# FFN1's pair stage: each product's token highs and lows in one 512-column matmul, and its modulation chunks on GpSimd

## The chip, the cores and the metric

The kernel runs on one NeuronCore of a Trainium2 chip. The metric is the device time of one execution in microseconds (us); lower is better. The inputs lie in HBM in float32.

## What is computed

The kernel is one layer of a diffusion backbone over 256 latent and 256 context tokens with 2048 channels. Two parts matter here. The first feed-forward network, for latent and context tokens with the same weights (inner size 5632, so 44 blocks of 128 rows):

```python
def swiglu(h, w_in, w_out):
    g, u = jnp.split(h @ w_in, 2, axis=-1)
    return (jax.nn.silu(g) * u) @ w_out

m_lat = (jax.nn.silu(c) @ ada_w[l] + ada_b[l]).reshape(b, N_MOD, 1, d)
x = x + 0.5 * m_lat[:, 2] * swiglu(modulate(rms_norm(x, norm1_g[l]), m_lat[:, 0], m_lat[:, 1]), ffn1_w_in[l], ffn1_w_out[l])
```

And the modulation vectors: a product of one vector silu(c) with ada_w (2048 x 18432), of which the later parts are formed little by little beside other work.

## The kernel before, in words

**Precision.** A float32 operand is split into a high part (float32r) and a low part, the rest. A product is three matmuls: weight high by token high, weight high by token low, weight low by token high (`three`, lines 1536 to 1540). ScalarE (ACT) makes the highs by a copy, VectorE (DVE) the lows by a subtraction.

**The stage.** FFN1's first layer has 44 blocks. Blocks 0 to 7 are done in the plain way. Blocks 8 to 43 (`for k in range(FIRST_S, PAIRS)`) are the pair stage, 36 rounds, each called a pair k here: gate and up of both token groups by a scheme of Strassen's kind with seven products (P1, P5, P6, P3, P7, P2, P4) in place of eight. Each product has 8 contraction tiles of 128 and 256 token columns: `pair_product` (line 1635) issues 8 x 3 matmuls of 128x256. Its weights are half slabs of 128x1024: ACT makes the high (`form_high_half`, line 1045), DVE the low (`half_low`, line 2455). Four half slabs of room exist, so the high of product n waits until product n-4 is done. P5 and P6 need weight sums that DVE forms in place (`w_sum`, line 2459, twice a pair), P7 and P4 weight sums that two accumulating DMAs issued by GpSimd form (`sums_added`, lines 862 and 865).

**Banks.** A pair has three PSUM banks x, y, z, and pairs alternate between two sets. x takes P1, then P6, P7 and P4 on top; z takes P5, then P3; y takes P2. Between them results are saved: `pair_keep` on ACT (line 1052) copies x after P1, z after P5 and x after P6, and PE waits for the first copy before P6, for the second before P3, for the third before P7. DVE's `up_ctx` (line 2467) reads x after P7, and PE waits for it before P4. `up_lat` (2472) and `gate_lat` (2476) read z and y. `pair_silu` (1060, 1062) applies SiLU to the two gates, and `pair_gate` (2482) multiplies gate and up into the activation, which GpSimd stores to DRAM (`act_store`, 856).

**Chunks.** Beside it DVE works through `chunk_step` (line 2315): a chunk is 128x1024 of ada_w, multiplied by one column of silu(c) and added to `accl`, one scalar_tensor_tensor. The stage has 96 chunks, 3, 3, 2 and 3 in four pairs, and so on (`S_CHUNKS`), over 35 pairs: 26 pairs with three, 9 with two. Sixteen chunks make a round, whose sums `take_turn`, `take_reduce` and `take_total` fold. Chunks are loaded by SP into three places; the load of a chunk waits for `chunk_free` of the one three before.

**Order.** All orders are written out by hand. In a pair DVE does: half_low 0, up_ctx of the pair before, w_sum, half_low 1, w_sum, gate_lat of the pair before, half_low 2, half_low 3, pair_gate of the pair before, then chunk and half_low in turn for 4, 5, 6, then up_lat. GpSimd's queue holds, per pair: the DMA for P7 (waits for the first w_sum of this pair), the DMA for P4 (waits for half_low 2), the store of the pair before (waits for pair_gate). SP's queue holds four half-slab loads for pair k+2 and the chunk loads between them.

Of the kernel before, what the change touches and what calls it, by code (L numbers as in the profile page):

```python
# [14 lines left out]
F32R = mybir.dt.float32r  # L15
# [5 lines left out]
P = 128  # L21
D = 2048
KT = D // P
# [105 lines left out]
def build(nc, x, c, ctx, c_ctx, ada_w, ada_b, norm1_g, ffn1_w_in, ffn1_w_out, norm2_g,  # L129
# [22 lines left out]
    def sm(name, shape, dt=F32):  # L152
# [7 lines left out]
    hh = at("hh", [P, 2, KT, LAT], F32R, o_hh)  # L160
    hl = at("hl", [P, 2, KT, LAT], F32R, o_hl)
# [5 lines left out]
              for part, n in enumerate(("ah", "al")))  # L167
    fhs, fls = ([at(f"{n}{k}", [P, HALF, LAT], F32R, o + part * 8 * KB) for k, o in enumerate((o_xl, o_xl + 16 * KB, o_a))]
                for part, n in enumerate(("fhs", "fls")))
# [197 lines left out]
    p7_summed, p4_summed = far_loaded, nfb_loaded  # L367
    lat_done, lat_out, LAT_DONE = xra_ready, xrv_ready, 8
# [150 lines left out]
    with block:  # L519
# [323 lines left out]
        def _(pool):  # L843
# [43 lines left out]
        def _(se):  # L887
# [166 lines left out]
            def pair_silu(k):  # L1054
                se.wait_ge(slab_used, prod(k, 6) + 1)
# [4 lines left out]
                nc.scalar.activation(sg[:, LAT:TOK], pair_banks(k)[0][:, 0:LAT], ACT.Silu).then_inc(a_x, 1)  # L1060
                se.wait_ge(a_c11, k - FIRST_S + 1)
                nc.scalar.activation(sg[:, 0:LAT], sg[:, 0:LAT], ACT.Silu).then_inc(a_sg, 1)

            for k in range(FIRST_S, PAIRS):
# [11 lines left out]
                pair_keep(k, 1, tv[:, 1, :], at_z, a_p5)  # L1076
                form_high_half(k, 5)
                pair_keep(k, 2, tv[:, 0, :], at_x, a_u2)
# [21 lines left out]
            act_high(1)  # L1100
            pair_silu(PAIRS - 1)
# [430 lines left out]
        def _(pe):  # L1532
# [102 lines left out]
            def pair_product(k, pos, bank_, first, last):  # L1635
# [4 lines left out]
                for t in range(HALF):  # L1640
                    if name in ("P1", "P2", "P4"):
                        part, t0 = {"P1": (0, 0), "P2": (0, HALF), "P4": (1, HALF)}[name]
                        xh_ap, xl_ap = hh[:, part, t0 + t, :], hl[:, part, t0 + t, :]
                    elif name == "P7":
                        xh_ap, xl_ap = hh[:, 1, t, :], hl[:, 1, t, :]
                    else:
                        f = ("P5", "P6", "P3").index(name)
                        xh_ap, xl_ap = fhs[f][:, t, :], fls[f][:, t, :]
# [1478 lines left out]
```

## Time and profile before

| | us |
|---|---|
| median of 3 runs (2681.79 to 2682.47) | 2681.8 |
| the profiled execution's own time | 2683.84 |
| its span, first to last instruction | 2682.0 |
| PE busy in the span | 2632.7 |
| DVE busy | 2134.1 |
| ACT busy | 1216.8 |
| GpSimd (POOL) busy | 93.7 |

PE is TensorE's matmuls, PEld its weight loads, DVE is VectorE, ACT ScalarE, POOL GpSimd, SP the queue that loads. A row of the timeline has the start from the span's begin, the duration, engine, line of the kernel, operation, output and input tile, shapes, and in brackets how long the engine had been idle and who released it. Durations of operations that follow each other overlap a little at the ends, so what one costs in a stream is read from start to start. The pair stage lies at about 287 to 1016 us.

### The profile page before, as it was taken

How to read it: one execution, taken by the hardware profiler on the slowest of the kernel's cores; microseconds unless marked ns; L12 is line 12 of the kernel's file. 1: busy time of each engine (PE TensorE's matmuls, PEld its weight loads, DVE VectorE, ACT ScalarE, POOL GpSimd, SP SyncE). 2: the span in 40 equal slices, each digit the busy share in tenths (PEclk: the TensorE clock that was granted, in tenths of full speed). 3: DMA queues.
4: the chain of work that ended last, by engine and by line, in shares of the span. 5: the costliest groups of instructions: out<-in, count | busy, mean ns of one | idle time of the engine just before them, and what ended most of it. 6: DMA issues, size and time to landing. Idle time of an engine off the chain costs nothing.

```text
span 2682.0 us, 37985 instructions
## 1 busy us (share of the span) xinstructions
PE 2632.7 (98%) x15293; PEld 2327.4 (87%) x15293; DVE 2134.1 (80%) x2328; ACT 1216.8 (45%) x1399; POOL 93.7 (3%) x131
## 2 busy tenths in 40 slices
PE   5999999999999999999999999999999999999998
PEld 4778999999999998888888988888988888888887
DVE  6869878788787877899797877586688888888866
ACT  6642344444444443231175543465465455555543
POOL 0000111111111110000000000000000000000000
PEclk9999999999999999999999999999999999999999
DMA  9967699999999888667584585442455555556463
GB/s 309 295 199 211 182 245 249 230 249 250 231 232 258 231 232 289 210 226 243 187 279 135 137 263 189 136 132 79 141 177 194 194 194 197 203 204 206 168 220 125
DMA packets 428939, 558.71 MB, mean 208 GB/s; under 512 B 22274, under 2 KB 280696, under 8 KB 428024
## 3 DMA queue, kind: packets, MB, share of 16 engines
q1 hardware_dynamic: 414156, 504.64, 58.4%
q0 software_dynamic: 14384, 51.92, 10.0%
q8 instruction: 104, 1.70, 0.3%
q14 instruction: 43, 0.35, 0.0%
q10 hardware_dynamic: 252, 0.10, 0.0%
HBM read 505.22 MB, written 13.63 MB: 193 GB/s over the span
## 4 chain that ended last, share of the span: by engine, by line
PE 87%; DVE 4%; ACT 1%; issue 1%; DMA 0%; ACTq 0%; DVEq 0%
PE py L1538 14%; PE py L1540 14%; PE py L1539 14%; PE pg L1538 3%; PE pg L1539 3%; PE pg L1540 3%; PE py L2071 3%; PE py L2073 3%; PE py L2072 3%; PE two L2013 2%; PE two L2015 2%; PE two L2014 2%; PE pu L2052 1%; PE pu L2054 1%; PE pu L2053 1%; PE pu L1538 1%
## 5 line engine op out<-in xcount | busy, mean ns | idle before, releaser
L2455 DVE TENSOR_TENSOR wl<-raw,wh 128x1024 fp32r<-128x1024 f32 x252 | 307.8, 1222 | 111.7 <-ACT wh L1045 111.5
L1045 ACT ACTIVATE wh<-raw 128x1024 fp32r<-128x1024 f32 x252 | 265.7, 1055 | 288.7 <-DVE raw L2459 228.0
L2176 DVE TENSOR_TENSOR wl<-raw,wh 128x2048 fp32r<-128x2048 f32 x101 | 231.1, 2288 | 124.4 <-ACT wh L902 124.2
L1538 PE MATMUL py<-ah,wh 128*128 128x512 f32 (+1 forms) x720 | 277.2, 385 | 0.3 <-issue 0.3
L1539 PE MATMUL py<-al,wh 128*128 128x512 f32 (+1 forms) x720 | 276.8, 384 | 0.0
L1540 PE MATMUL py<-ah,wl 128*128 128x512 f32 (+1 forms) x720 | 276.8, 384 | 0.0
L902 ACT ACTIVATE wh<-raw 128x2048 fp32r<-128x2048 f32 x100 | 190.7, 1912 | 189.0 <-PE py L1540 84.6
L1538 PE MATMUL py<-hh,wh 128*128 128x256 f32 (+1 forms) x752 | 226.1, 301 | 1.8 <-DVE hl L2253 1.0
L1539 PE MATMUL py<-hl,wh 128*128 128x256 f32 (+1 forms) x752 | 224.8, 299 | 0.0
L1540 PE MATMUL py<-hh,wl 128*128 128x256 f32 (+1 forms) x752 | 224.8, 299 | 0.0
L1538 PE MATMUL py<-fhs,wh 128*128 128x256 f32 x720 | 204.0, 283 | 0.4 <-DVE wl L2455 0.4
L1539 PE MATMUL py<-fls,wh 128*128 128x256 f32 x720 | 203.8, 283 | 0.0
L1540 PE MATMUL py<-fhs,wl 128*128 128x256 f32 x720 | 203.8, 283 | 0.0
L1096 ACT ACTIVATE wh<-raw 128x2048 fp32r<-128x2048 f32 x44 | 84.3, 1916 | 256.5 <-PE py L1540 256.4
L2315 DVE SCALAR_TENSOR_TENSOR accl<-chunk,cs,accl 128x1024 f32<-128x1024 f32 x150 | 191.9, 1280 | 7.4 <-DMA chunk<-in_ada_w 2.6
L1445 ACT ACTIVATE wh<-sraw 128x2048 fp32r<-128x2048 f32 x63 | 121.0, 1920 | 163.5 <-PE py L2073 59.4
L2945 DVE TENSOR_TENSOR wl<-raw,wh 128x2048 fp32r<-128x2048 f32 x70 | 160.0, 2286 | 35.3 <-ACT wh L1445 35.3
L2945 DVE TENSOR_TENSOR wl<-sraw,wh 128x2048 fp32r<-128x2048 f32 x63 | 144.1, 2287 | 50.3 <-ACT wh L1445 50.3
L1538 PEld LDWEIGHTS py<-ah,wh 128*128 128x128 f32 x720 | 135.3, 188 | 28.0 <-issue 0.9
L1538 PE MATMUL pg<-hh,wh 128*128 128x256 f32 (+1 forms) x528 | 158.1, 299 | 0.8 <-DVE tv L2467 0.6
L1540 PEld LDWEIGHTS py<-ah,wl 128*128 128x128 f32 x720 | 135.3, 188 | 26.8
L1539 PEld LDWEIGHTS py<-al,wh 128*128 128x128 f32 x720 | 135.3, 188 | 26.7
(516 smaller groups left out, 7124.9 us busy)
## 6 DMA issues: line engine op xcount, KB each, us to landing
raw<-in_ffn_w_out SPq DMA_DIRECT2D x84, 1024.0 KB, 5.2
chunk<-in_ada_w SPq DMA_DIRECT2D x160, 512.0 KB, 5.5
raw<-in_ffn_w_in SPq DMA_DIRECT2D x144, 512.0 KB, 7.5
raw<-in_ffn_w_in SPq DMA_DIRECT2D x58, 1024.0 KB, 5.1
sraw<-in_ffn_w_in SPq DMA_DIRECT2D x40, 1024.0 KB, 5.1
raw<-raw POOLq DMA_DIRECT2D x72, 512.0 KB, 5.8
raw<-in_ada_w SPq DMA_DIRECT2D x64, 512.0 KB
raw<-in_mix_w_in SPq DMA_DIRECT2D x30, 1024.0 KB
```

Source lines behind the costliest of these rows:

```text
L902: nc.scalar.activation(wh[:, slot % 2, :], raw[:, slot, :], ACT.Copy).then_inc(wh_ready, 1)
L1045: nc.scalar.activation(wh[:, slot, o:o + 1024], s_half(k, S_SRC[name]), ACT.Copy).then_inc(wh_ready, 1)
L1096: nc.scalar.activation(wh[:, j % 2, :], raw[:, slot, :], ACT.Copy).then_inc(wh_ready, 1)
L1445: nc.scalar.activation(whs[ring(i, name)], src, ACT.Copy).then_inc(wh_ready, 1)
L1538: mm(out_ap, w[0], xh_ap, start=first, stop=False, skip_group_check=True)
L1539: mm(out_ap, w[0], xl_ap, start=False, stop=False, skip_group_check=True)
L1540: return mm(out_ap, w[1], xh_ap, start=False, stop=last, skip_group_check=True)
L2071: mm(banks[k][:], xh_ap, w_h, start=(first and t == 0), stop=False)
L2176: tt(wl[:, slot % 2, :], raw[:, slot, :], wh[:, slot % 2, :].bitcast(F32), ALU.subtract).then_inc(wl_ready, 1)
L2315: ins = stt(a[:], chunks[PLACES[c]], cs[:, t, k:k + 1], a[:], ALU.mult, ALU.add)
L2455: tt(wl[:, slot, o:o + 1024], s_half(k, S_SRC[forms(k)[pos]]), wh[:, slot, o:o + 1024].bitcast(F32), ALU.subtract).then_inc(wl_ready, 1)
L2945: tt(wls[slot], src, whs[slot].bitcast(F32), ALU.subtract).then_inc(wl_ready, 1)
```

## The change

**Matmuls.** The high and low tokens of each operand become one tensor (`hhl`, `fhl`) at the same addresses, so that one access pattern reaches both. For each contraction tile `pair_product` issues two matmuls in place of three: weight high by [token high, token low] into all 512 columns of the bank, and weight low by token high into columns 0 to 255. The result is then the sum of the bank's two halves.

**Reads of the banks.** ACT's copies now take the right half; DVE then adds the left half to the copy (`both_halves`: keep_p1, keep_p5, keep_u2, gate_ctx) and releases PE. up_ctx, up_lat and gate_lat become two operations each with a wait between them. SiLU is one 512-column activation of both gates, after both are complete.

**Chunks.** The 96 chunks of the stage go to GpSimd: a tensor_scalar in place, a wait on its own semaphore, a tensor_tensor into `accl`. They stand in GpSimd's queue after the pair's store. The folding of a round stays on DVE, one pair later.

```diff
-    hh = at("hh", [P, 2, KT, LAT], F32R, o_hh)
-    hl = at("hl", [P, 2, KT, LAT], F32R, o_hl)
+    hhl = at("hhl", [P, 2, 2, KT, LAT], F32R, o_hh)
+    hh, hl = hhl[:, 0], hhl[:, 1]
...
+    fhl = [at(f"fhl{k}", [P, 2, HALF, LAT], F32R, o) for k, o in enumerate((o_xl, o_xl + 16 * KB, o_a))]
+    fhs, fls = ([f[:, part] for f in fhl] for part in range(2))
...
+            def chunk_step(c):
+                t = c % KT
+                pool.wait_ge(chunk_loaded[SIGNAL[c]], CHUNK_BASE[SIGNAL[c]] + 16 * LOADS[c])
+                pool.wait_ge(chunk_free, c + 1)
+                if t == 0:
+                    pool.wait_ge(sums_ready, (TAKEN[c // KT] - 1) * 5 + 1)
+                    ins = nc.gpsimd.tensor_scalar(accl[:], chunks[PLACES[c]], cs[:, 0, 0:1], None, ALU.mult)
+                else:
+                    nc.gpsimd.tensor_scalar(chunks[PLACES[c]], chunks[PLACES[c]], cs[:, t, 0:1], None, ALU.mult).then_inc(pool_chain, 1)
+                    pool.wait_ge(pool_chain, POOL0 + c - KT + 1 - c // KT)
+                    ins = nc.gpsimd.tensor_tensor(accl[:], accl[:], chunks[PLACES[c]], ALU.add)
+                ins.then_inc(chunk_free, 1)
             for k in range(FIRST_S, PAIRS):
                 sums_added(k)
                 act_store(k - 1)
+                for c in S_CHUNKS[k - FIRST_S]:
+                    chunk_step(c)
...
-            def pair_keep(k, pos, dst, src, ready):
+            def pair_keep(k, pos, dst, src):
                 se.wait_ge(slab_used, prod(k, pos) + 1)
-                nc.scalar.activation(dst, src[:, 0:LAT], ACT.Copy).then_inc(ready, 1)
+                nc.scalar.activation(dst, src[:, LAT:TOK], ACT.Copy).then_inc(kept, 1)
...
+                pair_keep(k, 6, sg[:, LAT:TOK], pair_banks(k)[0])
+
+            def pair_silu(k):
                 se.wait_ge(a_c11, k - FIRST_S + 1)
-                nc.scalar.activation(sg[:, 0:LAT], sg[:, 0:LAT], ACT.Silu).then_inc(a_sg, 1)
+                se.wait_ge(a_x, k - FIRST_S + 1)
+                nc.scalar.activation(sg[:], sg[:], ACT.Silu).then_inc(a_sg, 1)
...
                 if k > FIRST_S:
+                    keep_gate(k - 1)
+                form_high_half(k, 3)
+                if k > FIRST_S:
                     pair_silu(k - 1)
-                form_high_half(k, 3)
-                pair_keep(k, 0, p1a[:], at_x, a_p1)
+                pair_keep(k, 0, p1a[:], at_x)
...
-                    ins = three(bank_[:, 0:LAT], w, xh_ap, xl_ap, first and t == 0, t == HALF - 1)
+                    mm(pair(bank_[:]), w_h, both, start=(first and t == 0), stop=False, skip_group_check=True)
+                    ins = mm(bank_[:, 0:LAT], w_l, both[:, 0, :], start=False, stop=(t == HALF - 1), skip_group_check=True)
...
-                tt(tv[:, 1, :], tv[:, 1, :], pair_banks(k)[0][:, 0:LAT], ALU.subtract).then_inc(a_v, 1)
+                x_ = pair_banks(k)[0]
+                link(tt(tv[:, 1, :], tv[:, 1, :], x_[:, 0:LAT], ALU.subtract))
+                tt(tv[:, 1, :], tv[:, 1, :], x_[:, LAT:TOK], ALU.subtract).then_inc(a_v, 1)
...
+            def both_halves(k, n, dst, src, ready):
+                ve.wait_ge(kept, KEPT + 4 * (k - FIRST_S) + n)
+                tt(dst, src[:, 0:LAT], dst, ALU.add).then_inc(ready, 1)
...
                     gate_lat(k - 1)
-                    for c_ in span[:-3]:
-                        chunk_step(c_)
+                    for c_ in S_CHUNKS[k - FIRST_S - 1]:
                         if ends_round(c_):
                             take_turn(c_, 0)
                     half_low(k, 2)
...
+                    gate_ctx(k - 1)
                     half_low(k, 3)
                     pair_gate(k - 1)
...
+                    for n in range(3):
+                        (keep_p1, keep_p5, keep_u2)[n](k)
                         half_low(k, 4 + n)
```

## Rows read from the trace of the kernel before

**Rows 1.** The page: the span, and busy time by engine.
```profile
span 2682.0 us, 37985 instructions
PE 2632.7 (98%) x15293; PEld 2327.4 (87%) x15293; DVE 2134.1 (80%) x2328; ACT 1216.8 (45%) x1399; POOL 93.7 (3%) x131
```

**Rows 2.** Windows: stretch, length, busy by engine (instructions), granted clock, DMA share, GB/s.
```profile
320.00:860.00 540.00, 540.00 (x4503) 540.00 (x4502) 434.94 (x477) 233.62 (x321) 61.73 (x81) 1.00 0.94 243
...
40.00:80.00 40.00, 32.29 (x144) 24.57 (x143) 30.88 (x38) 26.13 (x21) 0.00 (x0) 0.96 0.88 289
```

**Rows 3.** Timeline of DVE, from one pair_gate to the next, the middle left out.
```profile
837.51 0.68 DVE L2482 TENSOR_TENSOR act<-sg,tv 128x512 f32<-128x512 f32 x1
838.12 1.28 DVE L2315 SCALAR_TENSOR_TENSOR accl<-chunk,cs,accl 128x1024 f32<-128x1024 f32 x1
...
848.84 0.42 DVE L2467 TENSOR_TENSOR tv<-tv,py 128x256 f32<-128x256 f32 x1 [0.57 <-PE py L1540]
849.18 1.22 DVE L2459 TENSOR_TENSOR raw<-raw 128x1024 f32<-128x1024 f32 x1
851.52 1.23 DVE L2455 TENSOR_TENSOR wl<-raw,wh 128x1024 fp32r<-128x1024 f32 x1 [1.13 <-ACT wh L1045]
852.66 1.22 DVE L2459 TENSOR_TENSOR raw<-raw 128x1024 f32<-128x1024 f32 x1
853.80 0.42 DVE L2476 TENSOR_TENSOR sg<-py,p1a 128x256 f32<-128x256 f32 x1
855.01 1.23 DVE L2455 TENSOR_TENSOR wl<-raw,wh 128x1024 fp32r<-128x1024 f32 x1 [0.79 <-ACT wh L1045]
856.53 1.23 DVE L2455 TENSOR_TENSOR wl<-raw,wh 128x1024 fp32r<-128x1024 f32 x1 [0.30 <-ACT wh L1045]
857.67 0.68 DVE L2482 TENSOR_TENSOR act<-sg,tv 128x512 f32<-128x512 f32 x1
```

**Rows 4.** Timeline of GpSimd (POOL), the same pair.
```profile
838.50 0.58 POOL L856 DMA_DIRECT2D act_scratch<-act  x1 [1.28 <-DVE act L2482]
850.69 0.86 POOL L862 DMA_DIRECT2D raw<-raw  x1 [11.61 <-DVE raw L2459]
856.53 0.85 POOL L865 DMA_DIRECT2D raw<-raw  x1 [4.98 <-DVE wl L2455]
858.66 0.58 POOL L856 DMA_DIRECT2D act_scratch<-act  x1 [1.28 <-DVE act L2482]
```

**Rows 5.** Timeline of PE: 256-column matmuls of a pair, then 512-column ones of FFN1's second layer.
```profile
1000.13 0.28 PE L1540 MATMUL py<-fhs,wl 128*128 128x256 f32 x1
...
1003.13 0.28 PE L1538 MATMUL py<-fhs,wh 128*128 128x256 f32 x1
...
1449.78 0.39 PE L1540 MATMUL py<-ah,wl 128*128 128x512 f32 x1
...
1452.72 0.39 PE L1538 MATMUL py<-ah,wh 128*128 128x512 f32 x1
```

**Rows 6.** Timeline of ACT around the end of the same pair.
```profile
855.45 1.05 ACT L1045 ACTIVATE wh<-raw 128x1024 fp32r<-128x1024 f32 x1
857.41 0.39 ACT L1052 ACTIVATE p1a<-pg 128x256 f32<-128x256 f32 x1 [0.91 <-PE pg L1540]
```

**Rows 7.** Timeline of DVE: the turn of a round's sums.
```profile
884.77 1.32 DVE L2327 STREAM_TRANSPOSE two<-accl 128x512 f32<-128x512 f32 x2
```

**Rows 8.** Line 881, GpSimd's one longer computation in the kernel before.
```profile
L881 POOL MEMSET yn<- x1: 3512/3512/3512, 1957.3 to 1957.3; 128x4096 f32 x1
```

**Rows 9.** Groups of DVE in 320 to 860 us: line, tiles, count | busy, mean ns | idle before.
```profile
L2455 DVE TENSOR_TENSOR wl<-raw,wh 128x1024 fp32r<-128x1024 f32 x189 | 230.9, 1222 | 85.6 <-ACT wh L1045 85.6
```

**Rows 10.** Line 2313, DVE's one-input multiplication of a round's first chunk.
```profile
L2313 DVE TENSOR_SCALAR accl<-chunk,cs x3: 725/728/728, 421.9 to 782.5; 128x1024 f32<-128x1024 f32 x3
```

**Rows 11.** Line 862, the DMA for P7: from issue to landing, 36 of them.
```profile
DMA to landing us min/median/max: 4.5/6.0/9.1
```

**Rows 12.** Line 1591: the longest wait of PE at the start of the kernel.
```profile
PE two L1591 <- DVE wl L2176: 19.5, 9, 6.7
```

More of the change, by code:

```diff
@@ L367, in build @@
     p7_summed, p4_summed = far_loaded, nfb_loaded
+    kept, KEPT = mods_ready, BLOCKS
+    pool_chain, POOL0 = rows_turned, BLOCKS
     lat_done, lat_out, LAT_DONE = xra_ready, xrv_ready, 8
@@ L1075, in _ @@
                     se.wait_ge(act_ready, k)
-                pair_keep(k, 1, tv[:, 1, :], at_z, a_p5)
+                pair_keep(k, 1, tv[:, 1, :], at_z)
                 form_high_half(k, 5)
-                pair_keep(k, 2, tv[:, 0, :], at_x, a_u2)
+                pair_keep(k, 2, tv[:, 0, :], at_x)
                 if k == FIRST_S:
@@ L1100, in _ @@
             act_high(1)
+            keep_gate(PAIRS - 1)
             pair_silu(PAIRS - 1)
@@ L2471, in up_lat, with keep_p1, keep_p5, keep_u2 @@
                 ve.wait_ge(slab_used, prod(k, 3) + 1)
-                tt(tv[:, 0, :], pair_banks(k)[2][:, 0:LAT], tv[:, 0, :], ALU.subtract).then_inc(a_t12, 1)
+                z_ = pair_banks(k)[2]
+                link(tt(tv[:, 0, :], z_[:, 0:LAT], tv[:, 0, :], ALU.subtract))
+                tt(tv[:, 0, :], z_[:, LAT:TOK], tv[:, 0, :], ALU.add).then_inc(a_t12, 1)
             def gate_lat(k):
                 ve.wait_ge(slab_used, prod_of(k, "P2") + 1)
-                tt(sg[:, 0:LAT], pair_banks(k)[1][:, 0:LAT], p1a[:], ALU.add).then_inc(a_c11, 1)
+                ve.wait_ge(a_p1, k - FIRST_S + 1)
+                y_ = pair_banks(k)[1]
+                link(tt(sg[:, 0:LAT], y_[:, 0:LAT], p1a[:], ALU.add))
+                tt(sg[:, 0:LAT], y_[:, LAT:TOK], sg[:, 0:LAT], ALU.add).then_inc(a_c11, 1)
+            def both_halves(k, n, dst, src, ready):
+                ve.wait_ge(kept, KEPT + 4 * (k - FIRST_S) + n)
+                tt(dst, src[:, 0:LAT], dst, ALU.add).then_inc(ready, 1)
+            def keep_p1(k):
+                both_halves(k, 1, p1a[:], pair_banks(k)[0], a_p1)
+            def keep_p5(k):
+                both_halves(k, 2, tv[:, 1, :], pair_banks(k)[2], a_p5)
+            def keep_u2(k):
+                both_halves(k, 3, tv[:, 0, :], pair_banks(k)[0], a_u2)
+            def gate_ctx(k):
+                both_halves(k, 4, sg[:, LAT:TOK], pair_banks(k)[0], a_x)
             def pair_gate(k):
@@ L2498, in _ @@
                     last_form(2)
+                    keep_p1(k)
                     half_low(k, 4)
+                    keep_p5(k)
                     half_low(k, 5)
                     form_lo(3)
+                    keep_u2(k)
                     half_low(k, 6)
@@ L2510, in _ @@
                     half_low(k, 2)
[L2511 to L2513 removed]
+                    gate_ctx(k - 1)
                     half_low(k, 3)
                     pair_gate(k - 1)
[L2516 to L2531 removed]
+                    for n in range(3):
+                        (keep_p1, keep_p5, keep_u2)[n](k)
+                        half_low(k, 4 + n)
+                        for c_ in S_CHUNKS[k - FIRST_S - 1]:
+                            if ends_round(c_) and n < 2:
+                                (take_reduce, take_total)[n](c_, 0)
                 up_lat(k)
@@ L2547, in _ @@
             act_low(1)
+            gate_ctx(PAIRS - 1)
             pair_gate(PAIRS - 1)
             down_low(1)
+            for c_ in S_CHUNKS[-1]:
+                if ends_round(c_):
+                    take_turn(c_, 0)
+                    take_reduce(c_, 0)
+                    take_total(c_, 0)
             def add_out(j, ds=range(4)):
```

33 lines of the change are left out of this document (5 added, 28 removed).

## The prediction

> **What bounds the kernel now.** The page comes first: PE is busy 2632.7 us of a span of 2682.0 [rows 1], so only PE's own work, or a new wait of PE, moves the time. The windows come next: in the steady part of the pair stage, 320 to 860 us, PE is busy 540.00 of 540.00 us with 4503 matmuls at granted clock 1.00, DVE 434.94 us (81%), GpSimd 61.73 us, all of it issuing DMAs, and the DMA engines 0.94 [rows 2]. 540/4503 is 0.120 us for a matmul, a product is 24 of them, 2.88 us, a pair 7 products, 20.16 us. The timelines of DVE and GpSimd show the same period: pair_gate at 837.51 and 857.67, the stores at 838.50 and 858.66 [rows 3, 4]. DVE runs ahead of PE, waiting for ACT here and there; PE waits for nobody. The profiled execution took 2683.84 us for its span of 2682.0; the median is 2681.8, so 2.0 us come off the sum at its end.
>
> **Matmuls.** 256-column matmuls start 0.120 us apart (25 of them in 3.00 us), 512-column ones 0.226 us apart (13 in 2.94 us) [rows 5]. By columns alone the second would be double; each instruction so carries 2 x 0.120 - 0.226 = 0.0135 us that don't depend on its columns. The change keeps the columns (512 + 256 for 3 x 256) and removes one instruction in three: 36 pairs x 7 products x 8 tiles = 2016 instructions, 27.2 us. A product takes 8 x 0.3465 = 2.77 us, a pair 19.40. That is all the change can gain: 0.76 us a pair. The Trainium skill (TensorE: Matmul & The Clock Gate, Back-to-back issue gap) gives columns/2.4 + 2.5 ns for the gap on the warm clock; the same 2016 instructions would then be worth an estimated 5 us. The trace doesn't agree with the 2.5 ns, and the measured gaps decide.
>
> **DVE.** Per pair it loses 2.74 chunk steps of 1.28 [rows 3] (96 chunks over 35 pairs), 3.5 us. It gains seven reads of a bank at 0.42 each (four first adds to ACT's copies, and a second operation in up_ctx, up_lat and gate_lat) [rows 3], 2.9 us, and three waits between linked operations; the trace shows no such wait between two of these, so 0 to 0.1 us each, 0.06 taken. DVE's total hardly changes: about 16 of 19.4 us, at the cost of its order, which now waits for PE and ACT at seven places. ACT: four copies and one SiLU in place of three copies and two SiLUs, even, at under half its time.
>
> **A new link in PE's waits.** PE needs P1's saved copy before P6, one product (2.77 us) after P1's end. Until now that was ACT's copy alone, 0.39 us from 857.41 [rows 6]. Now DVE's add follows, behind pair_gate in DVE's order. pair_gate ended at 858.35 [rows 3]; two more adds stand before it (gate_lat's second, gate_ctx), so 859.2, and keep_p1 ends at 859.6, against a deadline of 857.4 + 2.77 = 860.2: it fits by 0.6 us. Where a round's turn, 1.32 us [rows 7], is put before half_low 2, it is late by 0.7 us: six rounds, 4 us. The other waits have over 1 us.
>
> **Chunks on GpSimd.** The trace has no elementwise operation of GpSimd with an input. Nearest is the memset of 4096 columns in 3.51 us [rows 8], 0.88 us for 1024. Lower end: DVE's speeds, a two-input operation of 1024 columns 1.22 us [rows 9] and a one-input one 0.73 [rows 10], 1.95 us a chunk. Upper end: every operand and result passes at the memset's rate one after another, 1.76 + 2.64 = 4.4 us. I take the middle, 3.2 us (1.0 + 2.2), with the waits between the two inside. The Trainium skill (GPSIMD Engine Reference, Elementwise side-by-side cycle accounting) gives 4497 ns for a tensor_tensor of 2048 columns, so an estimated 2.25 us for 1024; no row here shows it.
>
> **Where they lie.** GpSimd takes its chunks between the store of the pair before, which waits for pair_gate, and the DMA for P7, which now stands behind them. That gap is 850.69 - 838.50 - 0.58 = 11.6 us [rows 4], 10.9 in a shorter pair, and three chunks take 9.6. P7's DMA may also come late: it lands 6.0 us after its issue [rows 11], at 856.7; ACT has to reach its weights by the end of P6 (863.1) less high 1.05, copy 0.39 and add 0.42, by 861.2 [rows 6]. So running beside each other, the chunks are hidden, up to some 4.5 us each.
>
> **What decides: do GpSimd and DVE run beside each other?** In the kernel before they never do on SBUF inputs, so no row says. Nine of DVE's operations a pair (seven half_lows, two w_sums) and pair_gate read two tiles of SBUF: 9 x 1.22 + 0.68 = 11.7 us. If such an operation and one of GpSimd's exclude each other, a pair falls into two stretches. A, from the first w_sum to pair_gate's end, is 849.18 to 858.35, 9.2 us, with DVE's two new adds 10.0; GpSimd can't start a chunk in it. B, from there to the next w_sum, holds the store's issue 0.6, four half_lows 4.9, and three chunks 9.6 or two 6.4, one after another, with the one-input adds beside GpSimd's turns: 15.1 or 11.9. A + B is 25.1 or 21.9 us; 26 pairs of the first and 9 of the second, mean 24.3. GpSimd's last operations may lie in A's waits for ACT (1.13 + 0.79 [rows 3]), up to 1.9 us off; half of it taken, 23.3. Against 20.16 that is +3.1 us, over 35 pairs +110; the first pairs start with DVE ahead and the two-chunk pairs catch up a little, so +100. Ends: 1.95 us a chunk gives +10, 4.4 gives over +190.
>
> The Trainium skill has this rule (SBUF — State Buffer, Who interferes with whom): a VectorE instruction with two SBUF inputs and a GpSimd instruction that reads SBUF share a read interface, held for a whole instruction, the later one fully blocked. It speaks against the change; by it the sum is the one above, without it the next case's. No row here shows it.
>
> **Rivals.** *Forecast: they take turns*, 2683.84 + 98 - 2 = about 2780; own range 2700 to 2860. For it: the gain is 0.76 us a pair, while 8.8 us of GpSimd's work move beside 11.7 us of DVE's on the same tiles' memory, in a loop (w_sum, high, low, gate, store, chunks, next DMA) with under 1 us of slack; a mutual delay of a fifth already costs more than the gain. Chance 0.64.
> *Side by side at full speed*: 27.2 - 4 - 2 for the first pairs, about -21, 2661. For it: a DMA's descriptors are issued beside DVE now without DVE slowing, 1.22 throughout [rows 9]. Against it: those don't read tiles. It holds up to 4.5 us a chunk. A DMA share of 0.94 would become 0.98 at the shorter pair, which could eat some. Chance 0.26.
> *GpSimd alone too slow*, no exclusion but over 4.5 us a chunk: P7's DMA is late, PE waits before P3; at 5 us a chunk a pair takes A's 8.0 us from P7's issue to the store plus 0.6 + 15, 23.6 with three chunks and 19.4 with two, mean 22.5, +82 less what the two-chunk pairs make up, 2750. Chance 0.05.
> *The new link*, DVE's add after ACT's copy, which overruns its 0.6 us in every pair by 1 us: +35 on the second case, 2696. Chance 0.05.
>
> A further cost of the first case is left in its range: PE's waits of several us. At the start PE waited up to 6.7 us at a time [rows 12] and the granted clock from 40 to 80 us was 0.96, part of it at the lower level, 1.2 GHz [rows 2]; 2% of a 730 us stage would be 15 us.
>
> **The numbers.** Predicted 2780. The range of 8 in 10 takes in the gain's case, from 2655, and the first case up to +170, 2850. Under 0.2% (5 us, what a measurement here can tell) is "same": faster 0.25, same 0.06, slower 0.69, the last from the first case 0.62, and parts of the others.
>
> **What would show it.** Right: in the steady windows PE busy under 90%, PE waiting for DVE's tv or p1a, ACT for the DMA raw<-raw; half_lows and w_sums beside GpSimd's chunks longer than 1.22 us or with idle time before them that no semaphore explains; three-chunk pairs longer than two-chunk ones. Wrong: DVE's two-input operations still at 1.22 us, stores 19.4 us apart, PE at 100%. The matmul term is right if a tile's two matmuls take 0.3465 us while PE doesn't wait.

## The result and the profile after

The changed kernel takes 2883.05 us in the median of 4 runs (2879.65 to 2884.88), the kernel before 2682.03 beside it: ratio 1.0748 (95% interval 1.0729 to 1.0766), 201 us slower. The forecast was 2780, its range ended at 2850. The profiled execution took 2884.88 us.

The page of the kernel after, against [rows 1]:

```profile
span 2883.1 us, 34369 instructions
PE 2681.2 (93%) x13277; PEld 2262.7 (78%) x13277; DVE 2245.1 (78%) x2484; ACT 1224.9 (42%) x1399; POOL 661.9 (23%) x317
```

PE has 2016 instructions fewer, as it should, and is busy 48 us *longer*, and there are 153 more microseconds in which it isn't busy (201.9 against 49.3). Windows of the kernel after, columns as in [rows 2]:

```profile
265.00:320.00 55.00, 47.13 (x232) 39.38 (x231) 44.72 (x60) 14.67 (x18) 3.74 (x5) 0.94 0.51 134
320.00:860.00 540.00, 446.43 (x2312) 381.24 (x2312) 397.99 (x455) 185.23 (x250) 388.52 (x174) 0.90 0.73 187
1260.00:2660.00 1400.00, 1393.37 (x6977) 1184.19 (x6976) 1126.41 (x1271) 650.37 (x756) 4.58 (x3) 1.00 0.57 187
```

In the pair stage PE is busy 83% of the time and its granted clock is 0.90, where both were full; behind the stage PE is full again, at granted clock 1.00. The stage's last store lies at 1222.5 us, before at 1019.9: the whole loss is in there. From store to store, pairs take 20.6 to 34.6 us, 25.8 in the mean of the 36, where they took 20.1 in the mean and 20.2 away from the rounds.

What GpSimd does, groups of its lines in 320 to 1220 us of the kernel after:

```profile
L879 POOL TENSOR_SCALAR chunk<-chunk,cs 128x1024 f32<-128x1024 f32 x60 | 206.0, 3434 | 6.9 <-POOL accl L881 6.0 <-POOL accl L877 0.5
L881 POOL TENSOR_TENSOR accl<-accl,chunk 128x1024 f32<-128x1024 f32 x60 | 159.9, 2665 | 5.0
L877 POOL TENSOR_SCALAR accl<-chunk,cs 128x1024 f32<-128x1024 f32 x4 | 14.1, 3517 | 26.1 <-DVE two L2349 26.0
```

A chunk is 3.4 + 2.7 us and the waits between, 6.3 us. The third row shows something else: first chunks of rounds waited 26 us for DVE's turn (`two`). The row holds four of the six rounds' first chunks; with those that read `accc`, four of the six waited, 32.8 us together (last row below). Waits in 320 to 1200 us of the kernel after (total, times, longest):

```profile
ACT wh L1062 <- DMA raw<-raw: 143.2, 37, 14.0
PE py L1671 <- DVE tv L2509: 97.5, 19, 13.6
PE py L1671 <- DVE p1a L2509: 37.3, 17, 2.9
POOL accl L877 <- DVE two L2349: 32.8, 4, 10.9
```

The chain of a pair with three chunks reads: GpSimd is late with P7's transfer, ACT waits for it (raw<-raw), DVE for ACT, PE for DVE's tv. It isn't the only one. In the same 320 to 1200 us P7's issue waits 14 times, 77.3 us in all, for DVE's w_sum, in 8 of them behind two chunks. And PE's waits for `p1a`, the new link, are no small thing: with those before a product into `pg`, there are 23 of them in 280 to 1222 us, 51.4 of PE's 156.3 us. GpSimd's timeline over one pair of three chunks, against [rows 4]:

```profile
709.84 0.59 POOL L858 DMA_DIRECT2D act_scratch<-act  x1 [1.21 <-DVE act L2527]
710.46 3.27 POOL L879 TENSOR_SCALAR accc<-accc,cs 128x1024 f32<-128x1024 f32 x1
713.81 2.41 POOL L881 TENSOR_TENSOR accl<-accl,accc 128x1024 f32<-128x1024 f32 x1
716.39 3.62 POOL L879 TENSOR_SCALAR chunk<-chunk,cs 128x1024 f32<-128x1024 f32 x1 [0.17 <-POOL accl L881]
...
726.37 2.96 POOL L881 TENSOR_TENSOR accl<-accl,chunk 128x1024 f32<-128x1024 f32 x1
729.27 0.89 POOL L864 DMA_DIRECT2D raw<-raw  x1
730.72 0.85 POOL L867 DMA_DIRECT2D raw<-raw  x1 [0.55 <-DVE wl L2477]
```

From the store to P7's issue it is 19.4 us; before it was 12.2 [rows 4], and there GpSimd had been waiting. Here P7's issue doesn't wait for anything: GpSimd reaches it late. ACT then waits, and PE when it resumes runs slowly (timelines of ACT and PE, same pair):

```profile
736.54 1.06 ACT L1062 ACTIVATE wh<-raw 128x1024 fp32r<-128x1024 f32 x1 [4.80 <-DMA raw<-raw]
```

```profile
740.19 0.50 PE L1671 MATMUL py<-fhl,wh 128*128 128x512 f32 x1 [2.71 <-DVE tv L2509]
740.53 0.32 PE L1672 MATMUL py<-fhl,wl 128*128 128x256 f32 x1
740.65 0.63 PE L1671 MATMUL py<-fhl,wh 128*128 128x512 f32 x1
741.08 0.41 PE L1672 MATMUL py<-fhl,wl 128*128 128x256 f32 x1
741.29 0.63 PE L1671 MATMUL py<-fhl,wh 128*128 128x512 f32 x1
```

From 740.65 to 741.29 a tile's two matmuls take 0.64 us, the lower level of 1.2 GHz; at full clock they take 0.347. Over 280 to 1222 us PE waits 156.3 us, in 49 places, and 404 matmuls are recorded longer than full-clock ones (over 0.47 us for 512 columns, over 0.33 for 256); the gaps from their starts to the next start are together 61.3 us longer than at full clock. That is worked out from all of PE's rows of the stage. The two together are 218 us; less the 9 to 14 us that the matmuls turn out to gain (below), they are about the loss, 201 us.

### The profile page after: what moved, and what is told of

It is laid out like the page before. It is cut to its first block, busy times and chain, and to the rows that moved or that the text cites. A ratio compares the mean times of both kernels' runs of the same rounds, so it can differ in the third digit from the quotient of the medians.

```text
span 2883.1 us, 34369 instructions
## 1 busy us (share of the span) xinstructions
PE 2681.2 (93%) x13277; PEld 2262.7 (78%) x13277; DVE 2245.1 (78%) x2484; ACT 1224.9 (42%) x1399; POOL 661.9 (23%) x317
## 4 chain that ended last, share of the span: by engine, by line
PE 64%; DVE 10%; POOL 8%; DMA 4%; issue 4%; ACT 3%; POOLq 0%; ACTq 0%; DVEq 0%
PE py L1560 8%; PE py L1562 8%; PE py L1561 8%; DMA raw<-raw 4%; PE py L1671 4%; POOL chunk L879 3%; DVE wl L2477 3%; PE py L2093 3%; PE py L2094 3%; PE py L2095 3%; POOL accl L881 3%; ACT wh L1062 2%; DVE raw L2481 2%; PE py L1672 2%; POOL accc L879 2%
## 5 line engine op out<-in xcount | busy, mean ns | idle before, releaser
L1671 PE MATMUL py<-fhl,wh 128*128 128x512 f32 x720 | 302.5, 451 | 127.9 <-DVE tv L2509 90.6
L1671 PEld LDWEIGHTS py<-fhl,wh 128*128 128x128 f32 x720 | 156.3, 217 | 178.0 <-DVE tv L2509 97.5
L919 ACT ACTIVATE wh<-raw 128x2048 fp32r<-128x2048 f32 x100 | 190.7, 1912 | 187.5 <-PE py L1562 84.6
L1672 PE MATMUL py<-fhl,wl 128*128 128x256 f32 x720 | 221.0, 307 | 0.0
L1671 PE MATMUL py<-hhl,wh 128*128 128x512 f32 x576 | 209.2, 405 | 8.3 <-DVE tv L2509 8.3
L879 POOL TENSOR_SCALAR chunk<-chunk,cs 128x1024 f32<-128x1024 f32 x60 | 206.0, 3434 | 6.9 <-POOL accl L881 6.0
L1117 ACT ACTIVATE wh<-raw 128x2048 fp32r<-128x2048 f32 x44 | 84.3, 1916 | 254.5 <-PE py L1562 253.0
L1672 PE MATMUL py<-hhl,wl 128*128 128x256 f32 x576 | 163.3, 284 | 0.0
L1671 PE MATMUL pg<-hhl,wh 128*128 128x512 f32 x432 | 156.4, 401 | 5.2 <-DVE tv L2509 4.1
L881 POOL TENSOR_TENSOR accl<-accl,chunk 128x1024 f32<-128x1024 f32 x60 | 159.9, 2665 | 5.0
L1672 PEld LDWEIGHTS py<-fhl,wl 128*128 128x128 f32 x720 | 157.5, 219 | 0.0
L1467 ACT ACTIVATE wh<-raw 128x2048 fp32r<-128x2048 f32 x70 | 134.0, 1914 | 53.3 <-PE py L2095 31.7
```

Of the source, the lines that this page charges most:

```text
L879: nc.gpsimd.tensor_scalar(chunks[PLACES[c]], chunks[PLACES[c]], cs[:, t, 0:1], None, ALU.mult).then_inc(pool_chain, 1)
L881: ins = nc.gpsimd.tensor_tensor(accl[:], accl[:], chunks[PLACES[c]], ALU.add)
L1467: nc.scalar.activation(whs[ring(i, name)], src, ACT.Copy).then_inc(wh_ready, 1)
L1671: mm(pair(bank_[:]), w_h, both, start=(first and t == 0), stop=False, skip_group_check=True)
L1672: ins = mm(bank_[:, 0:LAT], w_l, both[:, 0, :], start=False, stop=(t == HALF - 1), skip_group_check=True)
```

## Experiments

Each time is that of a single run unless a range is given; the kernel before took 2681.0 to 2682.2 us in the median beside each of them. The runs that were repeated spread over up to 7 us, so a step between two of these kernels is known to some 5 us. "Periods" are from one pair's store to the next.

### GpSimd without chunks, and what remains

**GpSimd without chunk work.** Each chunk is a memset of one column; all waits and signals stay.

```
-  nc.gpsimd.tensor_scalar(...); nc.gpsimd.tensor_tensor(...)
+  ins = nc.gpsimd.memset(chunks[PLACES[c]][:, 0:1], 0.0)
```

> The changed kernel with the stage's chunk arithmetic left out: GpSimd only clears one column of a chunk's place and hands it on (the modulation vectors are then not those of the reference). Folding, loads and matmuls stay. Theory 1 (all of the loss comes from the chunks on GpSimd): the matmul term is left, 27 us less PE's few waits behind DVE's new adds, 2660 us (2655 to 2668), PE full in the pair stage at 19.4 us a pair. Rival (the new link, DVE's add after ACT's copy, costs too): PE waits before P6 in most pairs, 2680 us or more.

Measured: 2714.7 us (2709.2 to 2716.2), ratio 1.0123 (1.0106 to 1.0140). Steady periods are 19.4 to 19.8 us, but four of the six rounds have one of 27 to 29, and the first pair takes 28.6 (before 21.0). So even with no work on GpSimd the change loses 33 us, and the theory (2660) fails; the rival's time comes true, but not by its cause: PE waits for p1a in two places, 6.8 us in the first pair and 2.7 in the second. GpSimd, PE and ACT at one round:

```profile
439.62 0.10 POOL L877 MEMSET chunk<- 128x1 f32 x1 [16.32 <-DVE two L2345]
440.13 0.85 POOL L864 DMA_DIRECT2D raw<-raw  x1 [0.41 <-issue]
...
448.32 1.06 ACT L1058 ACTIVATE wh<-raw 128x1024 fp32r<-128x1024 f32 x1 [6.41 <-DMA raw<-raw]
...
452.21 0.79 PE L1667 MATMUL py<-fhl,wh 128*128 128x512 f32 x1 [6.14 <-DVE tv L2505]
```

The first chunk of a round overwrites accl, so it waits until DVE's turn has read it. That turn stands behind the *next* pair's w_sum 0,2 in DVE's order (438.17), and P7's transfer of that next pair stands behind the chunk on GpSimd. Its data, DVE's first w_sum, were ready at 433.97; it was issued at 440.13.

**The same without that wait.** DVE's turn reads another tile (of hhl), so nothing orders it against the chunk; left out are the chunks and the rounds' sums.

```
-  pool.wait_ge(sums_ready, (TAKEN[c // KT] - 1) * 5 + 1)
-  nc.vector.transpose(b[:], accl[...])
+  nc.vector.transpose(b[:], hhl[...])
```

> The kernel without chunk arithmetic (e1), with the wait at a round's first chunk removed as well. Theory (each of five rounds costs 8 us by that wait ahead of P7's DMA): the pairs of 27 to 29 us become 20, the time 2670 to 2678 us. Rival (the fold itself, 4.6 us of DVE, makes them long): 2700 us or more.

Measured: 2677.94 us. The long periods at the rounds are gone (19.4 to 20.6): this wait costs 37 us against the median of the run before, 31 against its profiled execution (2709.2).

**The changed kernel without that wait**, its chunks kept, rounds' sums left out:

> The changed kernel without the wait at a round's first chunk: the fold of a round's sums reads another tile than the accumulator (so the modulation vectors are not those of the reference), and GpSimd's first chunk of a round waits no longer for DVE's turn of the sums. Theory (that wait stands ahead of P7's DMA in GpSimd's queue and holds up the loop): GpSimd's 39 us of idle time before line 877 go, the three longest pairs (34 us) come down to 28, and the time falls by 20 to 35 us, to about 2855. Rival (length of GpSimd's work alone): within 8 us of the changed kernel.

Measured: 2851.83 us, 33 less than the changed kernel's profiled execution. The wait costs about the same with the chunks as without them.

**And the first pair put right.** Against the run at 2677.94:

```
+  keep_p1(k)      # behind half_low 2
   last_form(1)
+  keep_p5(k)
   half_low(k, 3); std_mult(k - 1); last_form(2)
-  keep_p1(k)
   half_low(k, 4)
-  keep_p5(k)
```

> Edit, against the run with neither chunks nor round wait (2678 us): in the first pair VectorE adds the halves of P1 and P5 before it forms the last operands instead of after. Left out: the chunks, and a round's sum of them. Theory (the matmuls alone are worth what the forecast's term said, 27 us, once nothing new stands in front of them): the first pair falls from 28.3 to 22 to 23 us with the second at about 18.5, the clock of 265 to 320 us is 1.00 again, and the time is 2660 to 2672 us. Rival (the halves' additions give the gain back in some steady way that the first pair does not show): 2676 us or more.

Measured: 2673.5 us in the median (2668.2 to 2675.4), ratio 0.9970 (0.9957 to 0.9982). First pair 22.1 us, clock of 265 to 320 us 1.00. The matmul part is worth 8.7 us, where nothing else stands in its way (no chunk work lies on DVE either, so as a price of the matmuls alone this is if anything too good); the median lies between the two ranges, 1.5 us above the theory's. What PE waited for at the first pair without this edit (timeline of PE, the kernel with one-column memsets), DVE's add behind the forming of the last operands:

```profile
296.37 0.79 PE L1667 MATMUL pg<-fhl,wh 128*128 128x512 f32 x1 [6.84 <-DVE p1a L2505]
```

A tile's pitch, PE in the same kernel, and in the one with the chunks in DVE's gaps (below):

```profile
559.94 0.40 PE L1667 MATMUL pg<-hhl,wh 128*128 128x512 f32 x1
...
564.10 0.40 PE L1667 MATMUL py<-hhl,wh 128*128 128x512 f32 x1
```

```profile
559.70 0.40 PE L1669 MATMUL py<-fhl,wh 128*128 128x512 f32 x1
...
564.30 0.40 PE L1669 MATMUL py<-hhl,wh 128*128 128x512 f32 x1
```

12 tiles in 4.16 us are 0.3467 each, as forecast from [rows 5]; 13 in 4.60 are 0.3538. Both occur for stretches of several pairs, at granted clock 1.00 and without waits: periods of 19.4 and 19.8. What sets the one or the other wasn't found. In the profiled run of the last experiment, 2668.2 us, the stage ends 14.9 us earlier than before, not 27: 12 periods of 19.7 to 19.9 cost 5 us of it, the first two pairs, 22.1 and 19.0 for 21.0 and 17.4 before, 4 us against the forecast's steady gain, and the pairs at the rounds, 20.2 and 19.5 for 21.8 and 18.5, the rest.

### The chunks back on DVE

```
   for n in range(3):
       (keep_p1, keep_p5, keep_u2)[n](k)
+      chunk_step(span[n])     # DVE's, as before
       half_low(k, 4 + n)
```

> The changed kernel with its chunks back on DVE, placed as before: the matmul part alone. DVE's work, from start to start, is 7 lows and 2 sums at 1.14, the gate 0.61, 2.74 chunks at 1.19, three linked pairs at 0.8 and four adds at 0.34, with the folding about 18.8 us of a 19.4 us pair. Theory 1 (chunks on GpSimd are all of the loss): PE is nearly full, 2665 us (2658 to 2678), faster than before. Rival (DVE has no room, its order waits): three-chunk pairs take 20.5 us or more, 2690 to 2720 us.

Measured: 2697.3 us (2696.1 to 2699.4), ratio 1.0054 (1.0038 to 1.0071). Periods 19.8, at rounds 23.6, first pair 28.4: the rival's range.

**Chunks in DVE's gaps.** The first chunk between w_sum 0,1 and half_low 1, keep_p1 before pair_gate, the first pair as above, take_reduce and take_total one after each half_low.

> The changed kernel with its chunks on DVE, in other places: the first chunk of a pair between the first w_sum and half_low 1, where DVE waits 1.13 us for ACT; keep_p1 ahead of pair_gate; keep_p1 and keep_p5 early in the first pair; the fold one step after each half_low. Theory (in e2 DVE's order bound the three-chunk pairs at 19.8 us, with 1.13 us of waiting in it, and the first pair lost 10 us behind forming operands): pairs of 19.4 us, 2664 us (2658 to 2672), faster than before. Rival (DVE is full in any order): as e2, 2690 us or more.

Measured: 2682.01 us in the median of 10 runs (2679.5 to 2683.7), ratio 1.0000 (0.9990 to 1.0009). It is the best version that computes all, and it doesn't beat the kernel before, 10 us short of the theory's range. PE waits 15.1 us in the stage, in 18 places (2.8 in the kernel before); the first pair takes 22.4 us (21.0), the pairs at the rounds 21.1 to 23.1, and many others 19.8 instead of 19.4. That the seven more reads of banks meeting the chunks on DVE are what makes the rounds long is argued, not shown.

### The old matmuls, chunks on GpSimd

The matmuls, ACT's and DVE's order of the kernel before, with the change's chunk_step on GpSimd.

> The kernel before with only the chunk part of the change: three 256-column matmuls per tile and the old reads of the banks, chunks on GpSimd. Theory 1 (GpSimd's chunks bound the loop, matmuls don't matter): within 30 us of the changed kernel, 2850 to 2890 us. Rival (it needs both, the added waits of DVE for PE and ACT make the loop long): well under, 2780 us or less.

Measured: 2832.68 us, between the two ranges. GpSimd's chunks alone cost 151 us. The matmul part, put on top of them, costs another 50 where alone it gains. The two traces show where PE loses them. With the old matmuls PE waits 117.8 us in the stage (280 to 1171), and never for P1's saved copy, which ACT alone makes; in the changed kernel it waits 156.3, 51.4 of them for `p1a`, and its longer pitches are 61 us in place of some 33. One of these waits, timelines of DVE and GpSimd in the changed kernel:

```profile
678.80 2.84 DVE L2527 TENSOR_TENSOR act<-sg,tv 128x512 f32<-128x512 f32 x1
681.57 0.41 DVE L2509 TENSOR_TENSOR p1a<-py,p1a 128x256 f32<-128x256 f32 x1
```

```profile
677.79 3.30 POOL L881 TENSOR_TENSOR accl<-accl,accc 128x1024 f32<-128x1024 f32 x1
```

pair_gate reads two tiles, starts within GpSimd's addition and takes 2.84 us where it took 0.68 [rows 3]; keep_p1 stands behind it, and PE resumes at 682.0 after 2.7 us. So part of the 50 us is the new link's, made long by the taking of turns (next sections). Six of the 23 waits follow such a pair_gate; in 11 others one of DVE's 1024-column operations in the 9 us before took longer than alone (2.23 us at 728.19, before the wait that ends at 732.9). In the other six, two of them in the first two pairs, no operation is longer.

### How long may GpSimd take?

A chunk is 3, 4 or 6 memsets of 1024 columns, each waited for before the next; a round's first chunk has 3 in the last case. No input tile is read. Left out: the multiplication and the sum.

```
-  nc.gpsimd.tensor_scalar(...); nc.gpsimd.tensor_tensor(...)
+  for _ in range(2):          # 3, 5
+      nc.gpsimd.memset(accl[:], 0.0).then_inc(pool_chain, 1)
+      pool.wait_ge(pool_chain, ...)
+  ins = nc.gpsimd.memset(accl[:], 0.0)
```

> Edit, against the changed kernel: each chunk of GpSimd is three memsets of 1024 columns, one waited for after the other, about 3.1 us, the price that the forecast put on a chunk. Left out: the multiplication and the sum of the chunks. Theory (the gap of 10.9 us was judged rightly, and only the price was wrong): three take 9.3 us and are hidden, the pairs are those of the run without chunks, 19.4 to 19.8 with one of 27 to 30 a round, and the time is 2705 to 2725 us. Rival (work of GpSimd in this place delays the next pair at any length): pairs of three chunks of 21 us and more, over 2745 us.

> Edit, against the changed kernel: four such memsets a chunk, about 4.1 us; the same is left out. Theory (the transfer for P7 may come late by some 4 us before ACT misses it, so chunks are hidden up to 4.5 us): three take 12.3 us, delay the transfer by 1.4 us, and the time is that with three memsets, within 10 us. Rival (the transfer has no such slack, for what stands behind it is delayed too): pairs of three chunks of 21 us and more, and 25 us or more above the run with three memsets.

> The changed kernel with GpSimd's two operations per chunk replaced by six memsets of 1024 columns, each waited for (the chunks' arithmetic is left out). A memset reads nothing; six take about 5.8 us, a chunk's two operations 6.2. Theory A (GpSimd's length in the loop is the cost): about as slow as the changed kernel, 2850 to 2890 us, with DVE's lows at 1.22. Theory B (exclusion by reads is the cost): 2760 us or less.

Measured, with the median of the run without chunks in the first row (its profiled execution is 5 us shorter; waits of ACT for raw<-raw in 320 to 1050 us):

| us per chunk | time | against no chunks | ACT waits for raw<-raw |
|---|---|---|---|
| 0.1 | 2714.7 | | 33.8 |
| 3.1 | 2725.5 | +11 | 43.9 |
| 4.1 | 2736.7 | +22 | 88.0 |
| 6.1 | 2834.1 | +119 | 135.7 |

Up to 4.1 us the periods outside the rounds are 19.3 to 20.9; at 6.1 those of three chunks are 26 to 28.5 and those between them 19.9 to 21. With three memsets the time is at the upper end of what was expected, 2725, with four 11 us above that, just past the 10. Six come out 16 us under theory A's range and 74 over theory B's: the length is what counts, most of it. The forecast's gap, 10.9 us and some slack of the transfer, was judged nearly right; what it holds just isn't three chunks of 6. Past it the cost is steep, 97 us from 4.1 to 6.1 us a chunk; everything behind P7's issue (its landing 6 to 7 us later, ACT, DVE, PE) moves with it. With six memsets PE is busy 86% of the steady windows, at a clock of 0.92, though DVE has less to do than ever, 355 us (window of that kernel):

```profile
320.00:860.00 540.00, 465.06 (x2489) 399.40 (x2488) 355.35 (x485) 198.91 (x269) 392.17 (x425) 0.92 0.77 198
```

### Do GpSimd and DVE take turns?

The timeline of DVE after, same pair as in GpSimd's timeline above:

```profile
712.28 1.23 DVE L2477 TENSOR_TENSOR wl<-raw,wh 128x1024 fp32r<-128x1024 f32 x1 [0.52 <-ACT wh L1062]
715.06 2.24 DVE L2477 TENSOR_TENSOR wl<-raw,wh 128x1024 fp32r<-128x1024 f32 x1 [0.52 <-ACT wh L1062]
718.01 1.35 DVE L2477 TENSOR_TENSOR wl<-raw,wh 128x1024 fp32r<-128x1024 f32 x1
```

The first starts 1.8 us after the start of GpSimd's multiplication (710.46 to 713.73) and takes 1.23 us. The second starts within its addition (713.81 to 716.22) and ends 1.08 us after that one's end. The third starts 1.6 us into the next multiplication: 1.35. Over the stage, half_lows that start while GpSimd computes nothing take 1.23 us (107 of them), those that start within a multiplication 1.42 (94), within an addition 2.55 (51). In the group's mean, against 1222 ns [rows 9]:

```profile
L2477 DVE TENSOR_TENSOR wl<-raw,wh 128x1024 fp32r<-128x1024 f32 x243 | 383.4, 1578 | 184.1 <-ACT wh L1062 184.1
```

A multiplication holds DVE up too, but only by its first microsecond (timelines of GpSimd and DVE):

```profile
688.88 2.84 POOL L879 TENSOR_SCALAR chunk<-chunk,cs 128x1024 f32<-128x1024 f32 x1 [0.17 <-POOL accl L881]
```

```profile
689.41 1.66 DVE L2477 TENSOR_TENSOR wl<-raw,wh 128x1024 fp32r<-128x1024 f32 x1 [7.43 <-ACT wh L1062]
```

The half_low starts 0.53 us after the multiplication and ends 2.19 us after that start. Of 17 two-input operations of DVE that start in a multiplication's first 0.97 us, with none running before, 16 end 2.19 to 2.21 us after its start, whenever they began, and take 1.4 to 2.0 us; the 14 that start later take 1.21 to 1.23.

The multiplication is in turn held up by what DVE has running when it starts. It takes 2.84 to 2.97 us in 20 of the 22 cases in which DVE's two-input operation only starts within it, so such an operation beside it doesn't stretch it. In the 57 cases in which one is running at its start it takes 3.6 in the mean: 3.27 where that one ends 0.55 us after the start (the multiplication at 710.46, beside the half_low of 709.79 to 711.01), 3.62 where it ends 0.91 after (716.39, the half_low of 715.06). Where nothing of DVE's lies beside it, right behind the store's issue, it takes 2.86 or 3.48; that isn't explained. DVE's operations that read one bank and one tile (0.42) don't change.

**Additions alone.** GpSimd's tensor_scalar for t > 0 is left out, and so the factor of those chunks.

> The changed kernel with GpSimd's multiplications left out (so the sums are of unscaled chunks): one tensor_tensor a chunk. GpSimd's own work falls from 6.3 to 2.6 us a chunk, 7.9 us in a three-chunk pair, which alone fits its gap of 10.9 us. Theory A (length of GpSimd's work in the loop is all that counts): 2660 us. Theory B (its tensor_tensor and DVE's two-input operations exclude each other, and that costs on its own): DVE's lows beside it still take up to 3.4 us, and the time is 2710 to 2750 us.

Measured: 2763.18 us, 13 above theory B's range. A chunk is one addition, 2.95 us; DVE's half_lows:

```profile
L2475 DVE TENSOR_TENSOR wl<-raw,wh 128x1024 fp32r<-128x1024 f32 x242 | 423.1, 1748 | 93.3 <-ACT wh L1060 93.1
```

GpSimd is occupied as with three memsets (9.3 and 9.2 us for three chunks), yet the time is 38 us more: that is the taking of turns, with half_lows of 1748 ns.

**Multiplications alone**, the additions replaced by 2.5 waited memsets; left out is the chunks' sum.

```
-  ins = nc.gpsimd.tensor_tensor(accl[:], accl[:], chunks[PLACES[c]], ALU.add)
+  two waited memsets(accl[:]); ins = nc.gpsimd.memset(accl[:, 0:512], 0.0)
```

> Edit, against the changed kernel: GpSimd's multiplications stay as they are, its 90 additions are replaced by memsets of the same length (1024 + 1024 + 512 columns, waited for one after the other, some 2.4 us). Left out: the sums of the chunks. Theory (what holds VectorE up beside GpSimd is the addition of two SBUF tensors, not the multiplication): VectorE's two-input operations stay at 1.2 to 1.4 us beside every GpSimd instruction, the multiplication is stretched to about 3.4 us as before, and the time comes to that of the run with memsets alone, 2834 us, plus at most 25 us for the stretch: 2830 to 2860. Rival (every GpSimd instruction that reads SBUF costs VectorE the same): operations of 2 us and more beside the multiplications too, and 2875 to 2890 us.

Measured: 2832.08 us, as the theory said, the time of six memsets (2834.05). Groups in 320 to 1200 us:

```profile
L881 POOL TENSOR_SCALAR chunk<-chunk,cs 128x1024 f32<-128x1024 f32 x60 | 186.1, 3102 | 6.8 <-POOL accl L887 5.9 <-POOL accl L878 0.5
```

```profile
L2483 DVE TENSOR_TENSOR wl<-raw,wh 128x1024 fp32r<-128x1024 f32 x243 | 311.8, 1283 | 206.8 <-ACT wh L1068 206.8
```

In the mean DVE is hardly touched by multiplications, 1283 ns against 1222; the additions' taking of turns is the difference to the changed kernel, 51 us. It works both ways: three chunks occupy GpSimd 17.6 us here, 18.6 with six memsets, 19.5 in the changed kernel. And it reaches PE in good part through the new link: PE waits 12.6 us for p1a here, 9.7 with six memsets, 51.4 in the changed kernel, while its waits for tv hardly differ (116.5, 115.5, 104.0).

**A constant for the factor**, to see whether the scalar of each partition makes the multiplication slow:

```
-  nc.gpsimd.tensor_scalar(..., cs[:, t, 0:1], None, ALU.mult)
+  nc.gpsimd.tensor_scalar(..., 0.5, None, ALU.mult)
```

> Edit, against the changed kernel: GpSimd multiplies each chunk by the constant 0.5 instead of by a scalar of each partition. The modulation factor is left out. Theory (GpSimd reads one fp32 tensor times a scalar slowly in any form): the multiplication stays at 2.84 us alone, 3.4 us in the mean, and the time at 2875 to 2890 us. Rival (the scalar read from SBUF makes it slow, and without it the multiplication costs what a memset of as many columns does, 0.96 us): a chunk of 3.5 us, three of them almost in the gap of 10.9 us, and 2740 to 2790 us.

Measured: 2863.67 us; the shortest multiplications take 2.78 us, the mean is 3.2. The rival falls; the time is 11 us under what the theory gave.

### Another place in GpSimd's order

A pair's first chunk behind P7's issue instead of behind the store; everything is computed.

```
   pool.dma_start(s_half(k, 1), s_half(k, 2), accum_op=ALU.add)   # P7
+  chunk_step(S_CHUNKS[k - FIRST_S][0])
   ...
-  for c in S_CHUNKS[k - FIRST_S]:
+  for c in S_CHUNKS[k - FIRST_S][1:]:
```

> Edit, against the changed kernel: nothing left out; in GpSimd's own order a pair's first chunk comes after the P7 transfer is issued and only the others come after the store, so that three chunks no longer lie in one gap. Theory (the place in the queue is most of the loss: three chunks of 6.3 us in a gap of 10.9 us delay the next pair's P7 transfer by 8 us, and the round's first chunk waits for VectorE ahead of that transfer): pairs of three chunks fall from 27 to 28 us to 22 to 24, those of a round from 34 to 24, all pairs to 22 to 24, and the time to 2770 to 2820 us. Rival (the sum of GpSimd's work and the mutual stretching of the two engines is the bound, wherever the chunks stand): the mean pair stays over 25 us and the time over 2860 us.

Measured: 2859.09 us, with a mean period of 25.0: the theory fails, and the rival is met to within 1 us (it had said over 25 and over 2860). Outside the rounds most periods are 21.6 to 26.1, near what the theory said; but at the rounds they are 27 to 34, because the first chunk's wait for DVE's turn now holds up P4's transfer instead (GpSimd waits 60.7 us in 5 places for `two`, the longest 17.6). The place is worth only 24 us, for GpSimd's own work, about 2.7 chunks of 6.2 us and three issues, 19 us, fills the pair wherever it stands.

## Why the prediction was wrong

The direction was right, and so was the outline of the mechanism: GpSimd's chunks hold up the pair's loop, in part by taking turns with DVE. The weights were not. The forecast priced a chunk at 3.2 us, at which the chunks alone would be nearly hidden, and put the whole loss down to the turns; measured, most of it is the plain length of GpSimd's work, and the turns are a quarter. The size, 98 us over the kernel before, was half. The steps from kernel to kernel add up to the loss; the first holds two edits, the matmuls and the chunks' leaving DVE, the others one each, and where a number is of a single run it is good to some 5 us:

| from | to | step | us |
|---|---|---|---|
| before 2682.0 | matmuls alone, first pair and round wait out, 2673.5 | matmul part | -9 |
| 2673.5 | 2677.9 | first pair | +4 |
| 2677.9 | 2714.7 | round's wait ahead of P7's transfer (31 by the profiled executions) | +37 |
| 2714.7 | 2834.1 | GpSimd occupied 6.1 us a chunk | +119 |
| 2834.1 | 2883.1 | additions take turns with DVE, largely through p1a | +49 |

Point by point:

- **Matmuls, -27.2.** The pitch of 0.3465 us is right (0.3467), but in a third of the pairs it is 0.354, and the first pairs and the rounds don't gain. Alone the part gives 9 (14 in the profiled run). In the changed kernel it gives nothing, since PE isn't the bound. By the Trainium skill (TensorE: Matmul & The Clock Gate, Back-to-back issue gap), weighed there, the same instructions were worth an estimated 5 us; the pitch of 0.3467 doesn't agree with its gap. That the 9 us left over lie nearer to 5 than to 27 comes from the places just named, which take some 13 us back, and from what the single profiled run and the median differ by.
- **The price of a chunk, 3.2 us, with 4.4 as upper end.** This is the first step that failed, and the one that cost most. It is 6.3, of which the two operations undisturbed are 5.2 and the rest the turns and waits. The addition was well bounded: 2.34 us at least, taken 2.2. The estimate from the Trainium skill (GPSIMD Engine Reference, Elementwise side-by-side cycle accounting) was 2.25, and the trace agrees to 0.1 us. The multiplication was taken at 1.0 and is 2.84, more than the addition of two tensors; the bound "every operand and result at the memset's rate" gives it 1.76 and isn't a bound. The rival "GpSimd alone too slow" had this mechanism, over 4.5 us a chunk, and 0.05; its 2750 for 5 us lies between the measured 2736.7 at 4.1 us and 2834.1 at 6.1, which contain the 41 us of the two steps ahead of them in the table.
- **The gap, hidden up to 4.5 us a chunk.** Right as the place of the bend, but not quite hidden before it: +11 at 3.1, +22 at 4.1.
- **They take turns.** Right for the additions: DVE's half_lows go from 1.22 to 2.55 us. Right by half for the multiplications, which wait for the operation that DVE has running (3.27 and 3.62 us instead of 2.84), but hold DVE up only in their first microsecond. The rule weighed there (the Trainium skill, SBUF — State Buffer, Who interferes with whom) agrees with the additions' rows and with the multiplications that start second; for DVE's operations that start second beside a multiplication the trace doesn't show a wait for the whole instruction, since they end 2.19 us after the start of one that lasts 2.84. As a term: +49, not the 119 between the forecast's 2780 and its 2661 for running side by side.
- **The new link, +4, and "first pairs".** As a cost by itself it is right to the size of the spread: without GpSimd's work PE waits for p1a only in the first two pairs, 9.5 us. In the first, the order, keep_p1 behind three formings on DVE, costs 4 to 10 us; the forecast looked at the steady pairs alone. But the slack of 0.6 us was worked out without the turns. Beside them PE waits 51.4 us for p1a in 23 places, mostly under 3 us each, and not once with the old matmuls and the same chunks. The forecast had the two as rivals; in the changed kernel the one makes the other.
- **A wait that was missed.** The forecast never followed the round's first chunk: it waits for DVE's turn, and P7's transfer is queued behind it on GpSimd. It waits in four of the six rounds, +37 us (31 by the profiled executions), 33 with the chunks there. It was in the diff, and should have been walked past GpSimd's queue.
- **The clock, "some 15 us" left to the range.** 61 us of PE's longer pitches in the stage (44 with six memsets, 12 with none, 4 without the round's wait). It is no step of its own in the table above: it comes on top of the waits in each of them, 0.3 to 0.4 us for each microsecond that PE waits (61.3 for 156.3, 12.1 for 39.7).

## What to carry over

When work moves to another engine's queue, write down for each of its waits what stands behind it there: a wait that was harmless on DVE held a transfer on GpSimd that PE needed. Price an operation on an engine that has not done it by measuring it; here the operation with one input was the dearer one, near three times its assumed price, so the count of inputs is no guide. Once a gap is overrun, the cost isn't the overrun alone: behind 33 of PE's 34 waits of over 2 us in the stage came matmuls at half the clock. And work out a link's slack with the rivals' delays in it: 0.6 us held alone, and didn't beside the turns.

## What the runs showed of the hardware

- GpSimd multiplies 1024 columns of fp32 by a scalar in 2.84 us (2.78 by a constant) and adds two such tiles in 2.34 to 2.4; a memset of as many takes 0.96. The operation with one input is the slower one.
- In the changed kernel, a 1024-column operation of DVE with two SBUF inputs that starts within an addition of GpSimd ends 1.08 us after it. One that starts in the first 0.97 us of a multiplication ends 2.19 us after that one's start (16 of 17), a later one takes its 1.22 us. A multiplication that starts while such an operation runs takes 3.27 or 3.62 us, up to 4.7 behind two of them; one beside which it only starts takes 2.84 to 2.97 (20 of 22).
- DVE's operations with one input in PSUM and one in SBUF take 0.42 us throughout.
- After a wait of 2.71 us of PE, its matmuls ran at 0.64 us a tile instead of 0.347 for about 3 us (740.65 to 743.85), after one of 13.6 us for about 5 (796.88 to 802.13).
- Pairs of matmuls have two pitches at granted clock 1.00 without waits, 0.3467 and 0.3538 us a tile. This stays unexplained.
